# Stores of y and loads of the base x on GpSimd's queue instead of SyncE's, in a hybrid encoder layer

## The chip, the cores and the metric

The kernel runs on one core of a Trainium2 chip. The time is the device time of one execution in microseconds (us). Five engines run their own instruction streams and meet at semaphores: PE (TensorE, matrix products), DVE (VectorE), ACT (ScalarE), POOL (GpSimd) and SP (SyncE, which in this kernel only issues transfers). A transfer (DMA) is issued by one of these engines and carried out by the core's 16 DMA engines; SP's transfers run in a hardware queue (q1 in the profile) and POOL's in a software queue (q0).

## What is computed

One layer of a streaming encoder for 1024 prompt tokens and 64 tokens of a second request, width 1024, everything in float32:

```python
h = _rms(x, lw['norm1_g'])
proj = h @ lw['w_in']
p_rwkv, q, k, v, qm, gates = jnp.split(proj, _split_points(IN_SIZES), axis=-1)
...  # three mixers: a recurrence (o_a), windowed attention (o_b), attention into 256 memory tokens (o_m)
br = jnp.einsum('btnc,ncd->btnd', jnp.stack([o_a, o_b, o_m], axis=2), lw['w_branch'])
gt = jax.nn.sigmoid(gates.reshape(B, T, N_BRANCH, D_MODEL))
x = x + jnp.sum(gt * br, axis=2) @ lw['w_out']
h = _rms(x, lw['norm2_g'])
a_in, u = jnp.split(h @ lw['w_up'], 2, axis=-1)
...  # causal depthwise convolution of width 3 over a_in gives c
x = x + (jax.nn.gelu(c) * u) @ lw['w_down']
```

The input x is needed twice: normed, at the start, and unchanged, as the base to which the product with w_out is added. The sum (x1 in the kernel, and "x" in the profile, which drops numbers) takes the product with w_down on top and is the output y.

## The kernel before

Activations lie with the 1024 features on 8 tiles of 128 partitions and the tokens along the row. The tokens go through in three groups (GROUPS): 384, 384 and 320. For each group all weights are streamed from HBM again, in units: a unit is one output tile of 128 features, its weights 128 x 1024 floats (512 KB; half of that for w_branch, three quarters for w_down_end). A product in float32 is made of three in the faster fp32r form: ACT makes w_hi, a rounded copy of the raw weights (L318), DVE makes w_lo = raw - w_hi (L476), and PE adds hi*hi, lo*hi and hi*lo (L300, L301, L302) into one of two banks of `sums`. When PE is through with a unit, DVE or ACT reads its bank and so frees it for the unit after the next.

A group goes through these stages: attention columns (pa), in group 0 memory keys and values (mk, mv), recurrence columns (pr), then gates and branches, in pairs: a gate unit (512 KB), whose bank ACT reads with a tanh (L332), and a branch unit (256 KB), whose bank DVE multiplies by it (L512). The first sixteen pairs are for two branches (branch_first, branch), the last eight for the branch of the recurrence (branch_last), which needs the recurrence's result oa_hi, oa_lo (L1966, L1951). In the last eight pairs DVE adds to `merged` (L555) and ACT (L358) and DVE (L558) split it into mg_hi, mg_lo. Then the product with w_out (wo), 22 pairs with w_up (up_a, up_u), and 8 tiles with w_down, three units each (wd). DVE adds a finished tile of wo or wd to x1 (L516, L537).

Weights pass through a ring of four buffers `raw`. SP loads unit u + 3 when PE has finished unit u - 1 (`load`, L238): so a load is issued as PE starts a unit, and its data is wanted three units later. ACT's split of unit u + 2 stands in ACT's program ahead of what ACT does for the unit just finished.

The order of every engine is written out by hand: `in_order` (L2046) interleaves the steps of the small stages (norm, keys, attention, recurrence, base) with half units of the dense products, in the same way for each engine. Each engine holds only its own instructions, so an engine with nothing in a stretch goes on to its next instruction and waits there.

The lines in question:

- `store` in `dense_sync` (L241): after a tile's last w_down unit SP waits until DVE has added it to x1 (L244) and stores 128 x T floats of y (L245), T being the group's tokens. It stands behind the load of a later unit. There are 24 stores, of 192 KB in groups 0 and 1 and 160 KB in group 2.
- `base_sync` (L1970): SP waits for the group's last oa_lo and loads x again into x1, in four transfers of two tiles each (L1975; 384 KB, in group 2 320 KB). Its steps are interleaved with the last units of the gates, between the loads of their weights. DVE waits for all four ahead of wo (L515).
- `keys_pool` and `keys_in` (L837, L801): at the start of groups 1 and 2 POOL waits for the last store of y (L843), fills the attention's bias with a constant (L845) and loads the bias and the memory's keys and values (L816, L821, L824): 8 x 96 KB and 2 x 512 KB, in group 2 also 2 x 64 KB of cache.
- `end_sync` (L2028): SP stores two small outputs (o_cp, o_cs), behind all stores of y, and waits for the last transfers.

Of the kernel before, what the change touches and what calls it, by code (L numbers as in the profile page):

```python
# [45 lines left out]
GROUPS = ((0, 384), (384, 384), (768, 320))  # L46
# [142 lines left out]
def halves(n):  # L189
    return 2 if n.kt > 4 else 1  # L190
# [15 lines left out]
def freed(c, acc):  # L206

    return c.S["sum_free0" if acc % 2 == 0 else "sum_free1"], acc // 2 + 1
# [6 lines left out]
def raw_of(c, u):  # L215
    return c.raw[u % RAW_RING][:, 0:c.units[u].kt * P]
# [6 lines left out]
def lo_of(c, u):  # L223
    return c.w_lo[u % RAW_RING][:, 0:c.units[u].kt * P]


def dense_sync(sp, c):
    S = c.S
    loaded = [S[f"loaded{s}"] for s in range(RAW_RING)]

    def load(u):
        n = c.units[u]
        if u >= RAW_RING:
            sp.wait_ge(S["w_used"], u - RAW_RING + 1)
        dst = raw_of(c, u)
        if n.kind == "mv":
            dst = dst.rearrange("p (k m) -> p k m", k=2)
        sp.dma_start(dst, n.src).then_inc(loaded[u % RAW_RING], 16)  # L238

    def store(u):  # L240
        n = c.units[u]  # L241
        start = GROUPS[n.g][0]
        if n.kind == "wd" and n.ends:
            sp.wait_ge(*freed(c, n.acc))  # L244
            sp.dma_start(c.a["o_y"][:, n.m, start:start + n.T], c.x1[:, n.m, 0:n.T]).then_inc(S["y_out"], 16)  # L245

    for u in range(RAW_RING - 1):
        load(u)
    yield
    prev = None  # L250
    for u in c.sequence:
        if u is None:
            if prev is not None:
                store(prev)
            prev = None
            yield
            continue
        if u + RAW_RING - 1 < len(c.units):
            load(u + RAW_RING - 1)
        if halves(c.units[u]) == 2:  # L260
            yield
        if prev is not None:
            store(prev)
        prev = u
        yield


# [153 lines left out]
def dense_pool(pool, c):  # L421
    S = c.S

    def split(u):
        if u < len(c.units) and c.units[u].splitter == "pool":
            pool.wait_ge(S["w_hi"], u + 1)
            pool.tensor_tensor(lo_of(c, u), raw_of(c, u), hi_of(c, u).bitcast(F32), ALU.subtract).then_inc(S["w_lo_pool"], 1)

    def early(u):
        n = c.units[u]  # L430
        g, m, T = n.g, n.m, n.T
        i = FT * g + m
        if n.kind == "up_u":
            h = c.h[i % 2]
            pool.wait_ge(S["gelu"], i + 1)
            pool.wait_ge(*freed(c, n.acc))
            for tok, col in conv_parts(g):
                ins = pool.tensor_tensor(h[:, tok], h[:, tok], c.gl[i % 2][:, col], ALU.mult)  # L438
            ins.then_inc(S["h_made"], 1)
        if n.kind != "up_a":  # L440
            return
        raw = c.a_raw[i % 2]
        pool.wait_ge(*freed(c, n.acc))
        if g < LAST:
            pool.tensor_copy(c.conv_carry[:, 2 * m:2 * m + 2], raw[:, T:T + 2]).then_inc(S["carried"], 1)
        else:
            pool.tensor_copy(c.conv_carry[:, 2 * m:2 * m + 2], raw[:, PROMPT_END:PROMPT_END + 2])
            pool.tensor_copy(c.conv_last[:, 2 * m:2 * m + 2], raw[:, T + 2:T + 4]).then_inc(S["carried"], 1)

    split(0)  # L450
    split(1)
    yield
    prev = None
    for u in c.sequence:
        if u is None:
            if prev is not None:
                early(prev)
            prev = None
            yield
            continue  # L460
        if prev is not None:
            early(prev)
        if halves(c.units[u]) == 2:
            yield
        split(u + 2)
        prev = u
        yield
# [777 lines left out]
def idle(n):  # L1245
    for _ in range(n):
        yield
# [719 lines left out]
    yield from idle(2)  # L1967


def base_sync(sp, c, g):  # L1970

    start, T = GROUPS[g]
    sp.wait_ge(c.S["oa_lo"], 4 * (g + 1))
    for k in range(0, DT, 2):
        sp.dma_start(c.x1[:, k:k + 2, 0:T], c.a["xT"][:, k:k + 2, start:start + T]).then_inc(c.S["base_in"], 16)  # L1975
        yield


# [247 lines left out]
def build(nc, a):  # L2226
    c = Consts()
    c.a = a
    with ExitStack() as k:
        allocate(nc, c, k)  # L2230
        c.units, c.sequence = dense_units(c)
        c.acc = {(n.kind, n.g, n.m): n.acc for n in c.units if n.ends}
        block = k.enter_context(nc.Block())
        nothing = lambda steps: lambda g: idle(steps)

        def recurrence(eng, prep, inverse, state, post):
            def steps(g):
                yield from prep(eng, c, g)
                yield from scan(g, lambda p: inverse(eng, c, p), lambda p: state(eng, c, p))
                yield from post(eng, c, g)  # L2240
            return steps

        def together(eng, one, other):
            def steps(g):
                beside = other(eng, c, g)
                for _ in one(eng, c, g):
                    next(beside)
                    yield
            return steps

        def of(eng, step):
            return lambda g: step(eng, c, g)

        silent = lambda steps: lambda eng, c, g: idle(steps)

        @block.sync
        def _(sp):
            in_order(dense_sync(sp, c), {
                "first": lambda: first_sync(sp, c), "ready": lambda: idle(1), "start": lambda: start_sync(sp, c), "norm": of(sp, norm_sync), "memory": of(sp, memory_sync),
                "keys": nothing(KEY_STEPS), "attention": of(sp, attention_sync),  # L2260
                "recurrence": recurrence(sp, prep_sync, silent(INVERSE_STEPS), silent(STATE_STEPS), post_sync),
                "base": of(sp, base_sync), "norm2": nothing(1), "end": lambda: end_sync(sp, c)})

        @block.tensor
        def _(pe):
            in_order(dense_pe(pe, c), {
                "first": lambda: first_wait(pe, c), "start": lambda: idle(1), "ready": lambda: start_wait(pe, c), "norm": of(pe, norm_pe), "memory": of(pe, memory_pe),
                "keys": of(pe, keys_pe), "attention": of(pe, attention_pe),
                "recurrence": recurrence(pe, prep_pe, inverse_pe, state_pe, post_pe),
                "base": nothing(4), "norm2": of(pe, norm2_pe), "end": lambda: idle(1)})  # L2270

        @block.scalar
        def _(act):
            in_order(dense_act(act, c), {
                "first": lambda: first_wait(act, c), "start": lambda: idle(1), "ready": lambda: start_wait(act, c), "norm": of(act, norm_act), "memory": of(act, memory_act),
                "keys": of(act, keys_act), "attention": together(act, attention_act, mixing_act),
                "recurrence": recurrence(act, prep_act, inverse_act, state_act, post_act),
                "base": nothing(4), "norm2": of(act, norm2_act), "end": lambda: idle(1)})

        @block.gpsimd  # L2280
        def _(pool):
            in_order(dense_pool(pool, c), {
                "first": lambda: first_wait(pool, c), "start": lambda: idle(1), "ready": lambda: start_wait(pool, c), "norm": nothing(NORM_STEPS), "memory": nothing(MEM_STEPS),
                "keys": together(pool, keys_pool, keys_in), "attention": nothing(ATT_STEPS),
                "recurrence": recurrence(pool, prep_pool, inverse_pool, state_pool, silent(POST_STEPS)),
                "base": nothing(4), "norm2": nothing(1), "end": lambda: idle(1)})

        @block.vector
        def _(dve):
            in_order(dense_dve(dve, c), {  # L2290
                "first": lambda: first_wait(dve, c), "start": lambda: start_dve(dve, c), "ready": lambda: idle(1), "norm": of(dve, norm_dve), "memory": of(dve, memory_dve),
                "keys": of(dve, keys_dve), "attention": together(dve, attention_dve, mixing_dve),
                "recurrence": recurrence(dve, prep_dve, inverse_dve, state_dve, post_dve),
                "base": nothing(4), "norm2": of(dve, norm2_dve), "end": lambda: idle(1)})
# [144 lines left out]
```

## Time and profile before

| | us |
|---|---|
| median of 3 runs | 2136.65 |
| lowest and highest of them | 2132.02, 2137.83 |
| the profiled execution's own time | 2132.67 |
| its span in the trace | 2130.9 |

| engine | busy us | share of the span |
|---|---|---|
| PE | 2066.4 | 97% |
| DVE | 1264.5 | 59% |
| ACT | 945.4 | 44% |
| POOL | 165.6 | 8% |

The span is what the trace covers; the execution's own time holds 1.8 us more around it. Engine names with a q (SPq, POOLq) are an engine's queue of instructions that issue transfers. "To landing" is the time from the issue of a transfer until its semaphore has its full count. PE's matmuls overlap each other, so their busy times are merged in the share of the span. A window's row gives its width, then for each of PE, PEld (the weight load into the array), DVE, ACT and POOL the busy time and in brackets the number of instructions.

### The profile page before, as it was taken

What the parts mean: (1) busy time and instruction counts of PE and PEld (TensorE: products, weight loads), DVE (VectorE), ACT (ScalarE), POOL (GpSimd) and SP (SyncE); (2) the same over time, 40 slices, a digit from 0 to 9 for tenths busy, and PEclk for the clock granted to TensorE, in tenths of its full rate; (3) what the DMA queues carried; (4) which work ended last, traced back from release to release, by engine and by line L of the source; (5) the groups of instructions that cost most, each with busy time, mean ns of one, the idle gap of its engine ahead of it and who ended that gap; (6) DMA issues with size and microseconds to landing.
All of it is one profiled execution on the core that took longest, in us unless ns stands there. A gap on an engine that the chain in (4) does not pass through costs nothing.

```text
span 2130.9 us, 41128 instructions
## 1 busy us (share of the span) xinstructions
PE 2066.4 (97%) x17305; PEld 1963.6 (92%) x17305; DVE 1264.5 (59%) x2079; ACT 945.4 (44%) x1563; POOL 165.6 (8%) x268
## 2 busy tenths in 40 slices
PE   6999999999999999999999999999899999999999
PEld 5888899899999998889989999999888898999999
DVE  5566654656666545774446666654466645677753
ACT  5566332445444435743333544443475333455442
POOL 2000001001111010001000011100100110011110
PEclk9999999999999999999999999999999999999999
DMA  5422211354445452231124444455433213544454
GB/s 179 125 92 78 67 60 51 94 166 120 128 129 155 143 172 70 75 90 47 57 72 151 124 126 129 129 155 149 149 94 85 74 47 84 160 141 151 153 150 135
DMA packets 95959, 242.63 MB, mean 114 GB/s; under 512 B 24320, under 2 KB 35712, under 8 KB 95776
## 3 DMA queue, kind: packets, MB, share of 16 engines
q1 hardware_dynamic: 93984, 235.42, 36.9%
q0 software_dynamic: 1792, 4.59, 0.8%
q8 instruction: 137, 2.24, 0.4%
q14 instruction: 46, 0.38, 0.1%
HBM read 233.88 MB, written 6.09 MB: 113 GB/s over the span
## 4 chain that ended last, share of the span: by engine, by line
PE 87%; DVE 6%; ACT 3%; issue 2%; DMA 1%; SPq 0%; DVEq 0%; ACTq 0%
PE sums L300 24%; PE sums L302 23%; PE sums L301 23%; PE px L1491 5%; DVE w_lo L476 1%; PE px L1504 1%; PE ps_o L1041 1%; PE ps_o L1036 1%; PE pz L1767 1%; PE ps_t L1019 1%; PE ps_s L1005 1%; PE ps_s L1002 1%; DVE s L1120 1%; ACT w_hi L318 1%; PE ps_x L969 1%
## 5 line engine op out<-in xcount | busy, mean ns | idle before, releaser
L300 PE MATMUL sums<-x_hi,w_hi 128*128 128x384 f32 (+1 forms) x2208 | 742.3, 336 | 19.4 <-DVE x_lo L721 7.3
L302 PE MATMUL sums<-x_hi,w_lo 128*128 128x384 f32 (+1 forms) x2208 | 724.3, 328 | 0.0
L301 PE MATMUL sums<-x_lo,w_hi 128*128 128x384 f32 (+1 forms) x2208 | 724.2, 328 | 0.0
L476 DVE TENSOR_TENSOR w_lo<-raw,w_hi 128x1024 fp32r<-128x1024 f32 (+2 forms) x449 | 524.0, 1168 | 303.4 <-ACT w_hi L318 302.8
L318 ACT ACTIVATE w_hi<-raw 128x1024 fp32r<-128x1024 f32 (+1 forms) x452 | 441.0, 976 | 499.2 <-PE sums L302 273.4
L300 PEld LDWEIGHTS sums<-x_hi,w_hi 128*128 128x128 f32 x2208 | 417.7, 189 | 43.6 <-issue 29.4
L301 PEld LDWEIGHTS sums<-x_lo,w_hi 128*128 128x128 f32 x2208 | 418.5, 190 | 1.4
L302 PEld LDWEIGHTS sums<-x_hi,w_lo 128*128 128x128 f32 x2208 | 418.2, 189 | 0.0
L300 PE MATMUL sums<-h_hi,w_hi 128*128 128x384 f32 (+1 forms) x528 | 172.5, 327 | 0.0
L302 PE MATMUL sums<-h_hi,w_lo 128*128 128x384 f32 (+1 forms) x528 | 172.0, 326 | 0.0
L301 PE MATMUL sums<-h_lo,w_hi 128*128 128x384 f32 (+1 forms) x528 | 172.0, 326 | 0.0
L300 PE MATMUL sums<-o_hi,w_hi 128*128 128x384 f32 (+2 forms) x416 | 140.9, 339 | 4.8 <-DVE merged L512 3.6
L302 PE MATMUL sums<-o_hi,w_lo 128*128 128x384 f32 (+2 forms) x416 | 135.8, 326 | 0.0
L301 PE MATMUL sums<-o_lo,w_hi 128*128 128x384 f32 (+2 forms) x416 | 135.5, 326 | 0.0
L300 PEld LDWEIGHTS sums<-h_hi,w_hi 128*128 128x128 f32 x528 | 99.1, 188 | 0.2
L301 PEld LDWEIGHTS sums<-h_lo,w_hi 128*128 128x128 f32 x528 | 99.1, 188 | 0.2
L302 PEld LDWEIGHTS sums<-h_hi,w_lo 128*128 128x128 f32 x528 | 99.1, 188 | 0.0
L300 PEld LDWEIGHTS sums<-o_hi,w_hi 128*128 128x128 f32 x416 | 78.4, 189 | 10.5 <-issue 7.7
L438 POOL TENSOR_TENSOR h<-h,gl 128x384 f32<-128x384 f32 (+1 forms) x88 | 67.6, 779 | 231.5 <-DVE h L535 216.3
L365 ACT ACTIVATE gl<-cv 128x384 f32<-128x384 f32 (+1 forms) x66 | 33.6, 508 | 116.6 <-DVE cv L577 116.6
L577 DVE SCALAR_TENSOR_TENSOR cv<-a_raw,k_vecs,cv 128x384 f32<-128x384 f32 (+1 forms) x132 | 78.4, 594 | 2.3
L301 PEld LDWEIGHTS sums<-o_lo,w_hi 128*128 128x128 f32 x416 | 78.7, 189 | 0.7
(307 smaller groups left out, 2513.8 us busy)
## 6 DMA issues: line engine op xcount, KB each, us to landing
raw<-w_up SPq DMA_DIRECT2D x132, 512.0 KB, 3.6
raw<-w_gate SPq DMA_DIRECT2D x72, 512.0 KB, 3.6
raw<-w_down SPq DMA_DIRECT2D x48, 512.0 KB, 3.6
raw<-w_rwkv SPq DMA_DIRECT2D x42, 512.0 KB, 3.6
raw<-w_branch SPq DMA_DIRECT2D x72, 256.0 KB, 2.7
raw<-w_attn SPq DMA_DIRECT2D x30, 512.0 KB, 4.0
raw<-w_out SPq DMA_DIRECT2D x24, 512.0 KB, 3.6
raw<-w_down_end SPq DMA_DIRECT2D x24, 384.0 KB, 3.1
```

Source lines behind the costliest of these rows:

```text
L300: pe.matmul(out, wh[:, ws], n.hi[:, k, :], start=(n.begins and k == 0), stop=False)
L301: pe.matmul(out, wh[:, ws], n.lo[:, k, :], start=False, stop=False)
L302: mm = pe.matmul(out, wl[:, ws], n.hi[:, k, :], start=False, stop=(n.ends and k == n.kt - 1))
L318: act.activation(hi_of(c, u), raw_of(c, u), ACT.Copy).then_inc(S["w_hi"], 1)
L365: act.activation(c.gl[i % 2][:, 0:w], c.cv[i % 2][:, 0:w], ACT.Gelu_apprx_tanh).then_inc(S["gelu"], 1)
L438: ins = pool.tensor_tensor(h[:, tok], h[:, tok], c.gl[i % 2][:, col], ALU.mult)
L476: dve.tensor_tensor(lo_of(c, u), raw_of(c, u), hi_of(c, u).bitcast(F32), ALU.subtract).then_inc(S["w_lo_dve"], 1)
L577: dve.scalar_tensor_tensor(cv, raw[:, tap:tap + w], vec(c, "conv_w", 3 * m + tap), cv, ALU.mult, ALU.add).then_inc(S["conv"], 1)
L969: mm = pe.matmul(c.ps_x[0:nq, at:at + n], c.q_sq[:, i, tok], rhs, start=True, stop=True)
L1002: mm = pe.matmul(c.ps_s[0:p.nq, e, jj * 256 + cols.start:jj * 256 + cols.stop], c.q[H[e], 2 * p.r + jj, tok], c.kw[H[e], at + cols.start:a ...
L1005: mm = pe.matmul(c.ps_s[0:p.nq, e, jj * 256:jj * 256 + 256], c.q[:, 4 + 2 * e + jj, tok], c.mk[:, int(p.sample), 2 * e + jj, :], start=Tru ...
L1491: mm = eng.matmul(out[H[u], h * CHUNK:(h + 1) * CHUNK], tok(lhs, u, h), tok(rhs, u, h), start=True, stop=True)
```

## The change

The stores of y leave SP's program for POOL's, at the same place of the hand-written order; the loads of the base x do the same. Each keeps its wait. SP keeps the loads of weights, the next group's x for its norm, the tables and the small outputs.

```diff
 def dense_sync(sp, c):
...
-    def store(u):
-        n = c.units[u]
-        start = GROUPS[n.g][0]
-        if n.kind == "wd" and n.ends:
-            sp.wait_ge(*freed(c, n.acc))
-            sp.dma_start(c.a["o_y"][:, n.m, start:start + n.T], c.x1[:, n.m, 0:n.T]).then_inc(S["y_out"], 16)
...
@@ dense_pool
+    def store(u):
+        n = c.units[u]
+        start = GROUPS[n.g][0]
+        if n.kind == "wd" and n.ends:
+            pool.wait_ge(*freed(c, n.acc))
+            pool.dma_start(c.a["o_y"][:, n.m, start:start + n.T], c.x1[:, n.m, 0:n.T]).then_inc(S["y_out"], 16)
...
         if prev is not None:
             early(prev)
+            store(prev)
...
-def base_sync(sp, c, g):
+def base_in(pool, c, g):
 
     start, T = GROUPS[g]
-    sp.wait_ge(c.S["oa_lo"], 4 * (g + 1))
+    pool.wait_ge(c.S["oa_lo"], 4 * (g + 1))
     for k in range(0, DT, 2):
-        sp.dma_start(c.x1[:, k:k + 2, 0:T], c.a["xT"][:, k:k + 2, start:start + T]).then_inc(c.S["base_in"], 16)
+        pool.dma_start(c.x1[:, k:k + 2, 0:T], c.a["xT"][:, k:k + 2, start:start + T]).then_inc(c.S["base_in"], 16)
         yield
...
@@ block.sync
-                "base": of(sp, base_sync), "norm2": nothing(1), "end": lambda: end_sync(sp, c)})
+                "base": nothing(4), "norm2": nothing(1), "end": lambda: end_sync(sp, c)})
@@ block.gpsimd
-                "base": nothing(4), "norm2": nothing(1), "end": lambda: idle(1)})
+                "base": of(pool, base_in), "norm2": nothing(1), "end": lambda: idle(1)})
```

## Rows read from the trace of the kernel before

**Rows 1.** The page, part 1: busy time, share of the span, instructions.

```profile
PE 2066.4 (97%) x17305; PEld 1963.6 (92%) x17305; DVE 1264.5 (59%) x2079; ACT 945.4 (44%) x1563; POOL 165.6 (8%) x268
```

**Rows 2.** Windows, six stretches: width, busy us (count) per engine, clock, DMA, GB/s.

```profile
400.00:437.00 37.00, 37.00 (x208) 35.93 (x207) 24.48 (x40) 13.97 (x23) 0.00 (x0) 1.00 0.35 110
...
1154.00:1190.00 36.00, 35.91 (x206) 35.51 (x205) 21.66 (x32) 16.45 (x26) 0.00 (x0) 1.00 0.57 179
...
1390.00:1487.00 97.00, 97.00 (x561) 96.84 (x560) 48.00 (x66) 36.07 (x48) 1.50 (x3) 1.00 0.51 153
1487.00:1520.00 33.00, 31.35 (x211) 30.73 (x210) 14.06 (x20) 15.24 (x20) 8.69 (x13) 1.00 0.69 208
...
1815.00:1843.00 28.00, 26.54 (x179) 26.04 (x179) 17.25 (x29) 12.13 (x21) 0.00 (x0) 1.00 0.49 141
1843.00:1870.00 27.00, 25.10 (x168) 24.27 (x167) 16.45 (x25) 12.24 (x20) 0.00 (x0) 1.00 0.63 195
```

**Rows 3.** Timeline of DVE, group 0: start, duration, engine, line, operation.

```profile
406.66 1.96 DVE L1951 TENSOR_TENSOR oa_lo<-ar,oa_hi 128x384 fp32r<-128x384 f32 x4
```

**Rows 4.** Timeline of DVE, group 2, the same step.

```profile
1816.62 1.69 DVE L1951 TENSOR_TENSOR oa_lo<-ar,oa_hi 128x320 fp32r<-128x320 f32 x4
```

**Rows 5.** Timeline of SP's queue, group 0 (start, issue time).

```profile
412.17 0.33 SPq L238 DMA_DIRECT2D raw<-w_gate  x1
...
420.50 0.33 SPq L238 DMA_DIRECT2D raw<-w_branch  x1
...
437.54 0.43 SPq L1975 DMA_DIRECT2D x<-xT  x1
```

**Rows 6.** Timeline of ACT, group 0; in brackets the idle time before.

```profile
415.79 1.06 ACT L318 ACTIVATE w_hi<-raw 128x1024 fp32r<-128x1024 f32 x1 [2.54 <-DMA raw<-w_gate]
...
419.57 0.47 ACT L332 ACTIVATE th<-sums 128x384 f32<-128x384 f32 x1
```

**Rows 7.** DMA issues at 400 to 437: count, KB each, median us to landing.

```profile
raw<-w_gate SPq DMA_DIRECT2D x5, 512.0 KB, 3.5
```

**Rows 8.** Timeline of POOL, start of group 1.

```profile
774.19 4.70 POOL L816 DMA_DIRECT2D bias<-alibi  x8 [0.59 <-POOL bias L845]
...
779.45 0.56 POOL L824 DMA_DIRECT2D mv<-o_mv  x1
```

**Rows 9.** Timeline of DVE, the same stretch.

```profile
775.18 1.22 DVE L476 TENSOR_TENSOR w_lo<-raw,w_hi 128x1024 fp32r<-128x1024 f32 x1 [1.20 <-ACT w_hi L318]
```

**Rows 10.** DMA issues at 780 to 784 (issued at 781.73).

```profile
raw<-w_attn SPq DMA_DIRECT2D x1, 512.0 KB, 5.8
```

**Rows 11.** DMA issues at 784 to 788 (issued at 785.89).

```profile
raw<-w_attn SPq DMA_DIRECT2D x1, 512.0 KB, 4.4
```

**Rows 12.** DMA issues at 1496 to 1500 (issued at 1496.88).

```profile
raw<-w_attn SPq DMA_DIRECT2D x1, 512.0 KB, 6.7
```

**Rows 13.** Chain that ended last, 1815 to 1872: start, duration, what.

```profile
1820.89 3.54 DMA raw<-w_gate
...
1849.38 4.21 DMA raw<-w_gate
```

**Rows 14.** Timeline of PE in that stretch.

```profile
1828.66 0.39 PE L300 MATMUL sums<-x_hi,w_hi 128*128 128x320 f32 x1 [0.76 <-ACT th L332]
```

**Rows 15.** Tile bias, 770 to 900: ns min/median/max, first and last start.

```profile
L1120 DVE SCALAR_TENSOR_TENSOR s<-ps_s,q_y,bias x24: 473/476/485, 826.7 to 891.3; 128x256 f32<-128x256 f32 x24
```

**Rows 16.** Timeline at the end, all engines.

```profile
2127.46 0.49 DVE L537 TENSOR_TENSOR x<-sums,x 128x320 f32<-128x320 f32 x1 [7.49 <-PE sums L302]
...
2128.84 0.45 SPq L2032 DMA_DIRECT2D o_cs<-conv_last  x1
```

**Rows 17.** DMA issues at 2127.9 to 2128.3.

```profile
o_y<-x SPq DMA_DIRECT2D x1, 160.0 KB, 1.8
```

**Rows 18.** DMA issues at 2098 to 2129.

```profile
o_cs<-conv_last SPq DMA_DIRECT2D x1, 22.0 KB, 1.6
```

**Rows 19.** Tile bias, whole span, loads by POOL: us to landing.

```profile
DMA to landing us min/median/max: 2.7/3.8/5.4
```

More of the change, by code:

```diff
@@ L249, in dense_sync @@
     yield
-    prev = None
     for u in c.sequence:
         if u is None:
-            if prev is not None:
-                store(prev)
-            prev = None
             yield
@@ L261, in dense_sync @@
             yield
-        if prev is not None:
-            store(prev)
-        prev = u
         yield
@@ L462, in dense_pool @@
             early(prev)
+            store(prev)
         if halves(c.units[u]) == 2:
```

## The prediction

> **What bounds the kernel now.** I read the page's busy times first, then windows stage by stage, then, for the stages that the change touches, the chain of waits and the timelines. PE is busy for 2066.4 of 2130.9 us [rows 1], so a change off PE's path can win only where PE idles. The windows show where that is [rows 2]: in the w_down stage, where y is stored, PE idles 0 of 97 us (all three groups read 97.00). In the stage with the base loads it idles 0.09 us of 36 in group 1 (group 0 alike), but in group 2 1.46 of 28 us just before the loads and 1.90 of 27 during them. With 320 tokens PE needs less time for the same weights, and there the transfers set the pace: the chain runs through the landing of w_gate, 3.54 us after its issue [rows 13], then ACT's split, DVE's w_lo, the merge, and ACT's tanh that frees PE's bank; the next gate unit waited 0.76 us for that tanh [rows 14].
>
> **The change part by part.**
>
> *What leaves SP.* 24 stores and 12 base loads, each an issue of 0.33 to 0.43 us [rows 5]. SP's loads wait for PE to be done with an old buffer, and between two of them SP stands still for longer than an issue. So this frees nothing that PE waits for: 0.
>
> *The stores in the w_down stage, on POOL.* POOL has nothing else there (1.50 us busy of 97, PE full [rows 2]). A POOL issue takes 0.56 to 0.59 us (8 in 4.70) [rows 8]. The data of a store now shares the DMA engines with a weight load instead of standing behind it in one queue, which may delay that load a little; PE has no idle time in the stage, and its loads are wanted three units later. I take 0. DVE might be held while POOL issues: w_lo took 1.22 us in the middle of eight POOL issues [rows 9], its usual time, so 0 again. Behind the last store of a group POOL now fills the bias and loads it later, by about 0.25 us for the longer issue and 0.5 for the slower landing. The bias is first read at 826.7 [rows 15], its loads are issued from 774.19 [rows 8] and take 5.4 us at most [rows 19], so some 40 us cover this. The shift moves POOL's burst of bias and memory loads against w_attn's, a stretch where PE idles 1.65 of 33 us in group 2 [rows 2]; it may cost or give back up to 1.5 us, and I take 0.
>
> *The base loads on POOL.* This is the real move. SP issued them paced by PE, one to a unit, from 437.54 [rows 5], each behind a weight load in the same queue. POOL has no pace: in the gate stage it has no instruction (0.00 us, x0, from 400 to 437 [rows 2]), so it waits at the last oa_lo and issues all four at once. That wait ends in group 0 at 406.66 + 1.96 = 408.62 [rows 3], 29 us earlier than before. Nothing behind it on POOL is due before w_up, and DVE wants the data only at w_out, so early does no harm to them. But 4 x 384 KB now arrive in some 2.4 us of issues, in a separate queue, beside the loads of w_gate and w_branch.
>
> How much can a gate load be late? In group 0 the next one is issued at 412.17 [rows 5]. It landed by 415.79, when ACT split it; behind that hang w_lo, the merge, the next split and the tanh, which ended at 419.57 + 0.47 = 420.04 [rows 6]. PE ended the unit before at 420.50, when SP's next load was released [rows 5]. So 0.46 us are to spare; beyond, every late microsecond is PE's. Group 2 has nothing to spare [rows 14].
>
> How late will it be? The nearest rows are POOL's bursts at the start of groups 1 and 2: 8 x 96 and 2 x 512 KB from 774.19 to 780.0 [rows 8]. Loads of the same 512 KB from SP took 5.8 us when issued 1.7 us after the last of these issues, 4.4 us when issued 5.9 us after it, and at worst, between the two largest, 6.7 us [rows 10 to 12]; undisturbed, w_gate takes 3.5 [rows 7]. The base burst is smaller (1.5 MB against 1.8) and its last issue ends about 1.2 us ahead of the gate load. I take 5.2 us in groups 0 and 1, between the rows of 4.4 and 5.8 and nearer to the second: 5.2 - 3.5 - 0.46 = 1.2 us each. Only one gate load a group is hit: the next follows a pair of units later, some 6 us. In group 2 the wait ends at 1818.31 [rows 4], POOL's issues at about 1820.7, and the gate load goes out at 1820.89 [rows 13], closer: I take 5.5, with no spare 2.0 us. Against that, the old base loads no longer delay the gate load at 1849.38, which took 4.21 [rows 13]: minus 0.7. Net 1.3 us. Lower bound of the part: no load is delayed, 0 + 0 - 0.7; upper: each takes 6.7, 2 x 2.7 + 3.2 - 0.7 = 7.9.
>
> The Trainium skill has a rule for this, in "DMA: Bandwidth & Descriptors", "Queues, rings and completion order": each DMA engine takes turns between the queues that have work for it, a packet at a time. By it a gate load beside a burst gets half of the engines: if 2 of its 3.5 us are fixed (the page's fit, in "Anatomy of one DMA — SWDGE (gpsimd) path"), the other 1.5 double, and it lands after 5.0 us, an estimate; the sum of the three groups would be 1.0 + 1.0 + 0.8 = 2.8 us against 3.7. The rows of 5.8 and 6.7 lie above it, so the trace decides.
>
> *The end.* DVE ends the last tile at 2127.46 + 0.49 = 2127.95; SP then issued the store (landing after 1.8 us [rows 17]), and o_cp and o_cs behind it; o_cs ended the run, issued at 2128.84 [rows 16] and landed 1.6 later [rows 18], at 2130.44, 0.46 before the end of the span. Now o_cp and o_cs go out earlier, and POOL's store ends it. A landing of POOL's issues takes 2.7 us at least, 3.8 in the median, for 96 KB in busy stretches [rows 19]; the quiet store from SP took 1.8. I take 2.5: 2127.95 + 2.5 + 0.46 = 2130.9, so 0; bounds 1.8 and 3.8 give -0.7 and +1.3.
>
> By the Trainium skill, in that same section of "DMA: Bandwidth & Descriptors", 2.0 us and the bytes at 436 GB/s, the 160 KB land after 2.4 us, an estimate, and the end would come 0.1 earlier; no row here shows a quiet POOL store.
>
> *Sum:* 1.2 + 1.2 + 1.3 + 0 = 3.7 us; bounds -0.7 - 0.7 - 1.5 = -2.9 and 7.9 + 1.3 + 1.5 = 10.7. The profiled execution took 2132.67 us, 3.98 less than the median of the runs, whose times fall into one at 2132 and two near 2137. I add the sum to the middle of the two, 2134.7, and forecast 2138.4.
>
> **The rivals.**
>
> *A, the transfers hide anyway.* The burst's data is over before the gate load's begins, or POOL's transfers start so slowly that a gate load hardly notices. For it: the engines are busy only 35% of the time from 400 to 437 [rows 2], and the burst's issues end before the gate load's issue. Against: the landings of 5.8 and 6.7 [rows 10, 12], and a gate load has less spare than w_attn. Then 0 + 0 - 0.7 and the end: about -0.7, 2134.0. The Trainium skill, "DMA: Bandwidth & Descriptors", "Issuing engines are not separate DMA queues", goes this way: issuing from several engines saves only the issue time. The trace agrees as far as the issue time is hidden here, but not that the pace stays the same.
>
> *B, the freed stretch runs faster.* All that PE idles where base loads and weights shared SP's queue, 2 x 0.09 + 1.46 + 1.90 [rows 2], and 0.7 at the end come back: -4.2, 2130.5. Against: the 1.46 are lost before any base load is issued, so they have another cause.
>
> *C, slower: the burst holds w_gate for its full length.* Place: the gate load behind POOL's four issues, in each group. If it takes 6.7 us, as the worst row [rows 12], PE waits 2.7 + 2.7 + 3.2 - 0.7 and the end adds 1.3: +9.2, 2143.9. For it: that row, and 1.65 us that PE lost right behind it [rows 2]. Against: that load lay between two transfers of 512 KB, this one lies behind the last issue. It counts as slower from landings of about 6.2 us on.
>
> That the base loads keep their old times is no rival: nothing on POOL holds them until 437.
>
> **How the numbers follow.** Chances: forecast 0.50, A 0.29, B 0.05, C 0.16. A run of this kernel can be told from no change at about 0.3%, 6.4 us. The forecast's own range is 2134 to 2143. The range reaches down to A on the lower of the two levels, about 2131, and up to C with some of the spread of the runs, 2146. Faster by over 0.3%: B alone comes near, 0.03. Slower: most of C and a little of the forecast, 0.15. The rest, 0.82, is within 0.3%.
>
> **What would show it.** In the changed trace POOL issues four base loads back to back once a group, at about 408.7 in group 0 and 1818.4 in group 2; the next w_gate load lands after 5 to 6 us instead of 3.5, and PE waits for ACT's tanh once behind it, for about 1 us. In the w_down stage PE stays at 97.00 of 97. At the end o_cp and o_cs come before the last tile, and a POOL store is last. I am wrong if that gate load lands within 4 us (A), if it takes over 6.2 (C), or if PE idles in the w_down stage.

## The result, and the profile after

The changed kernel is slower: 2152.59 us in the median of six runs (2150.75 to 2155.34) against 2135.58 for the kernel before in the same rounds. The ratio is 1.0083 with a 95% interval of 1.0073 to 1.0093, a loss of 17.0 us between the medians. The prediction was 2138.4 with a range up to 2146.0 and a chance of 0.15 for slower by over 0.3%; the time lies outside the range.

The profiled execution took 2155.34 us, the longest of the six, with a span of 2153.5. Part 1 of its page, beside [rows 1]: PE is busy 8.2 us longer with the same 17305 instructions, so its matmuls have become slower, and that is not all of the loss.

```profile
PE 2074.6 (96%) x17305; PEld 1971.1 (92%) x17305; DVE 1265.0 (59%) x2079; ACT 945.3 (44%) x1563; POOL 189.7 (9%) x304
```

**The base loads.** POOL's timeline of the changed kernel in groups 0 and 2 (start, duration, engine, line, idle time before). The four loads go out back to back when oa_lo is done, as predicted, though each takes 0.73 us to issue and not 0.58.

```profile
409.48 2.92 POOL L1970 DMA_DIRECT2D x<-xT  x4 [39.26 <-DVE oa_lo L1946]
...
1831.16 2.93 POOL L1970 DMA_DIRECT2D x<-xT  x4 [45.28 <-DVE oa_lo L1946]
```

The DMA issues from 412 to 414 of the changed kernel (KB each, us to landing). The load of w_gate, issued at 412.74, took 6.8 us, where [rows 7] have 3.5.

```profile
raw<-w_gate SPq DMA_DIRECT2D x1, 512.0 KB, 6.8
```

The chains of waits that hold the same load in groups 1 and 2 of the changed kernel (start, duration), where [rows 13] have 3.54 and 4.21:

```profile
1136.11 6.33 DMA raw<-w_gate
```

```profile
1833.45 7.65 DMA raw<-w_gate
```

Three windows of the changed kernel show why (columns as in [rows 2]; the last two are the DMA engines' busy share and GB/s). From 412 to 418 the engines are full. The burst, this gate load and the branch load behind it are 1536 + 512 + 256 KB, 2.36 MB; at some 340 GB/s, from these rows, that is 6.9 us of work, an estimate, and the gate load lands when nearly all of it is done.

```profile
412.00:414.00 2.00, 2.00 (x14) 2.00 (x13) 1.44 (x3) 1.01 (x2) 0.40 (x1) 1.00 0.96 346
414.00:416.00 2.00, 2.00 (x13) 2.00 (x12) 0.71 (x2) 0.00 (x0) 0.00 (x0) 1.00 1.03 320
416.00:418.00 2.00, 2.00 (x13) 2.00 (x13) 0.00 (x0) 0.00 (x0) 0.00 (x0) 1.00 0.92 362
```

**The chain to PE.** ACT's timeline in the changed kernel: the split waits 5.77 us for the load, against 2.54 in [rows 6], and the tanh that frees PE's bank comes at 423.36 instead of 419.57.

```profile
419.59 1.06 ACT L304 ACTIVATE w_hi<-raw 128x1024 fp32r<-128x1024 f32 x1 [5.77 <-DMA raw<-w_gate]
...
423.36 0.47 ACT L318 ACTIVATE th<-sums 128x384 f32<-128x384 f32 x1
```

PE's timeline in the three groups of the changed kernel: the pause in brackets, and the first matmul behind it, which in group 2 takes 0.61 us against the 0.39 of [rows 14].

```profile
423.97 0.55 PE L286 MATMUL sums<-x_hi,w_hi 128*128 128x384 f32 x1 [2.94 <-ACT th L318]
...
1146.85 0.41 PE L286 MATMUL sums<-x_hi,w_hi 128*128 128x384 f32 x1 [2.45 <-ACT th L318]
...
1845.33 0.61 PE L286 MATMUL sums<-x_hi,w_hi 128*128 128x320 f32 x1 [4.87 <-ACT th L318]
```

Windows of the changed kernel behind each pause; the column ahead of the DMA share is the granted clock. It is about 0.50 (1.2 GHz) for some three us in groups 0 and 1 and six in group 2, and 1.00 (2.4 GHz) again afterwards; the windows of four us take in some of that. The time lost by it is the busy time by one minus the clock: 1.7 + 1.6 + 2.8 = 6.1 us, on top of the pauses' 2.94 + 2.45 + 4.87 = 10.3.

```profile
424.00:428.00 4.00, 4.00 (x14) 4.00 (x15) 2.89 (x5) 1.30 (x2) 0.00 (x0) 0.57 0.02 4
...
1147.00:1151.00 4.00, 4.00 (x15) 4.00 (x16) 2.77 (x5) 1.18 (x2) 0.00 (x0) 0.59 0.00 0
...
1845.00:1851.00 6.00, 5.67 (x22) 5.70 (x23) 3.10 (x5) 1.60 (x3) 0.00 (x0) 0.51 0.01 3
```

**The w_down stage** with its stores on POOL, a window of the changed kernel: PE is full, as in the 97.00 of [rows 2].

```profile
678.00:776.00 98.00, 98.00 (x566) 97.73 (x565) 49.78 (x66) 37.90 (x49) 5.65 (x11) 1.00 0.51 155
```

**The end.** The changed kernel's last rows of the timeline, where [rows 16] had a store by SP:

```profile
2146.45 0.49 DVE L532 TENSOR_TENSOR x<-sums,x 128x320 f32<-128x320 f32 x1 [7.38 <-PE sums L288]
2147.24 0.54 POOL L420 DMA_DIRECT2D o_y<-x  x1 [8.71 <-DVE x L532]
```

This store landed after 2.1 us, at 2149.3. The span goes on to 2153.5, since the program's end (L2224, the close of the block; L2229 before) has a DRAIN on POOL's queue. Instructions of that line, first in the changed kernel, then in the kernel before (durations in ns; first and last start):

```profile
L2224 POOLq DRAIN  x1: 6029/6029/6029, 2147.2 to 2147.2; - x1
```

```profile
L2229 POOLq DRAIN  x1: 4256/4256/4256, 2050.7 to 2050.7; - x1
```

Before, POOL was through with its program at 2050.7, and its 4.26 us lay beside the w_down stage. Now 6.03 us stand behind the last store. From the last tile's end to the end of the span (the tail, below) it was 2130.9 - 2127.95 = 2.95 us; now it is 2153.5 - 2146.94 = 6.6.

The account of the two profiled spans, 22.6 us apart: pauses 10.3, less the 0.76 that group 2 had before [rows 14], clock 6.1, end 3.6, together 19.2. Most of the other 3.4 us can be found too. Summed over windows of 2 us, PE's busy time by one minus the clock is 29.5 us after and 21.5 before, so the clock costs 8.0 us more, 1.9 of them away from the three pauses: for example behind a wait of 2.15 us for the recurrence's table from_rows at 1810.08, where before a wait of 2.12 us at 1799.10 left the clock at 1.00. And in the attention of group 2, where a load of w_attn now takes 7.63 us (at 1511.45), PE's pauses for DVE's q add up to 3.15 us against 2.38. The medians are only 17.0 us apart.

### The profile page after: what moved, and what is told of

The parts are those of the page before. It is cut to its first block, busy times and chain, and to the rows that moved or that the text cites. A ratio compares the mean times of both kernels' runs of the same rounds, so it can differ in the third digit from the quotient of the medians.

```text
span 2153.5 us, 41128 instructions
## 1 busy us (share of the span) xinstructions
PE 2074.6 (96%) x17305; PEld 1971.1 (92%) x17305; DVE 1265.0 (59%) x2079; ACT 945.3 (44%) x1563; POOL 189.7 (9%) x304
## 4 chain that ended last, share of the span: by engine, by line
PE 85%; DVE 6%; ACT 3%; DMA 2%; issue 2%; SPq 0%; POOLq 0%; POOL 0%; DVEq 0%; ACTq 0%
PE sums L286 23%; PE sums L288 22%; PE sums L287 22%; PE px L1486 5%; DMA raw<-w_gate 1%; DVE w_lo L471 1%; ACT w_hi L304 1%; PE px L1499 1%; PE ps_o L1036 1%; PE ps_t L1014 1%; PE pz L1762 1%; PE ps_s L1000 1%; PE ps_o L1031 1%; PE ps_s L997 1%; PE ps_x L964 1%
```

## The experiments

My theory was that the price is the burst, because POOL has no pace, and that the end adds the rest; the rivals were the software queue itself and the bytes brought early. Base and stores were parted first. All ratios are to the kernel before, timed on the same chip in the same rounds, with their 95% interval; the microseconds behind them are differences of the medians, which can differ from the ratio by a few tenths.

**stores_only**: the base loads go back to SP.

```diff
-                "base": of(pool, base_in), ...        # POOL
+                "base": of(sp, base_sync), ...        # SP, paced by its weight loads
```

> Stores of y on GpSimd's queue, base loads back on SyncE's. Theory (the four base loads in one burst make a w_gate load late in each group, PE stands still over 2 us and then runs at half its clock; the stores cost nothing but the end): the three stalls behind w_gate are gone, what stays is the end, 3 to 4 us longer because GpSimd's drain of 6.0 us follows the last store; time about 2139, 3 to 4 us over before. Rival (GpSimd's software queue slows the weight loads wherever it runs, the 24 stores too): PE idles in the w_down stage, and at least half of the 17 us stay, 2144 or more.

2138.1 against 2133.59 us, 1.0018 (1.0009 to 1.0027): 4.5 us. No gate load was late. The end line of this kernel, behind a last tile done at 2132.31 in a span of 2137.9:

```profile
L2224 POOLq DRAIN  x1: 5051/5051/5051, 2132.6 to 2132.6; - x1
```

The tail is 5.6 us instead of 2.95. For the other 1.9 us the profiled execution has a candidate, not a shown cause: PE waits 3.04 us for the recurrence's table at 1802.13 (2.12 before) and runs at half the clock for some three us behind it. last_store_on_sync, below, has 23 of the same stores and waits 1.97 us there.

**base_only**: the base loads on POOL, the stores still on SP.

> Base loads on GpSimd's queue, stores of y back on SyncE's. Theory: the three stalls stay (w_gate landing 6.3 to 7.6 us after its issue, PE idle 2.5 to 5 us each, clock 0.5 for 3 to 5 us after), the end is as before; about 13 to 15 us over before, 2149 to 2151. Rival (stores carry half of the loss): 2144 or less.

2147.26 against 2133.59, 1.0062 (1.0040 to 1.0084): 13.7 us, within the 13 to 15 over before that I expected, though the time lies below 2149, as the kernel before stood lower in these rounds. The gate loads took 6.3, 6.8 and 6.5 us, and PE paused 2.42, 2.91 and 3.68 us. The tail stayed at 2.9 us. PE's timeline and a window behind the first pause:

```profile
421.66 0.66 PE L300 MATMUL sums<-x_hi,w_hi 128*128 128x384 f32 x1 [2.42 <-ACT th L332]
```

```profile
421.66:425.00 3.34, 3.34 (x11) 3.34 (x12) 2.58 (x5) 1.32 (x2) 0.00 (x0) 0.50 0.03 9
```

So two parts, 13.7 + 4.5 = 18.2 us, make up the 17.0 of the whole, within the noise (the interval of base_only alone is 8.5 to 17.9 us).

**base_paced**: base_only, but POOL waits, ahead of each load, for the unit at which SP had issued it. It parts POOL's queue as such from the pace.

```diff
     pool.wait_ge(c.S["oa_lo"], 4 * (g + 1))
-    for k in range(0, DT, 2):
+    last = last_of(c, "branch_last", g) - 1
+    for k, v in zip(range(0, DT, 2), (last - 3, last - 2, last, last + 1)):
+        pool.wait_ge(c.S["w_used"], v - RAW_RING + 1)
         pool.dma_start(...)
```

> Base loads on GpSimd's queue but each held until PE reaches the unit at which SyncE issued it in the kernel before; stores on SyncE's queue. Theory (the pace is what was lost, not the queue): the w_gate loads land after 3.5 to 4.5 us, no stall of over 1 us, time within 3 us of before, 2134 to 2139. Rival (a transfer in the software queue beside a weight load delays it by itself, since it no longer stands behind it): gate loads at 5 to 6 us in the last two pairs of each group and 2142 or more.

2132.53 against 2133.59, 0.9997 (0.9987 to 1.0008). POOL's timeline shows the loads apart, and a window shows PE full:

```profile
437.01 0.75 POOL L1977 DMA_DIRECT2D x<-xT  x1 [68.06 <-PE sums L302]
438.83 0.73 POOL L1977 DMA_DIRECT2D x<-xT  x1 [1.06 <-PE sums L302]
445.07 0.72 POOL L1977 DMA_DIRECT2D x<-xT  x1 [5.51 <-PE sums L302]
449.23 0.72 POOL L1977 DMA_DIRECT2D x<-xT  x1 [3.44 <-PE sums L302]
```

```profile
400.00:440.00 40.00, 40.00 (x225) 38.85 (x224) 25.79 (x41) 14.85 (x26) 1.48 (x2) 1.00 0.41 117
```

The same loads on the same queue, without the burst, cost nothing. The queue is not the price.

**burst_on_sync**: the four loads at oa_lo, but issued by SP in its own queue.

```diff
+def base_now(sp, c, g):
+    sp.wait_ge(c.S["oa_lo"], 4 * (g + 1))
+    for k in range(0, DT, 2):
+        sp.dma_start(c.x1[:, k:k + 2, 0:T], ...).then_inc(c.S["base_in"], 16)
...
     yield from idle(POST_STEPS)
+    base_now(sp, c, g)
```

> Base loads stay on SyncE's queue, but all four are issued back to back as soon as the last oa_lo is there, as GpSimd did. Theory (the burst fills the DMA engines; in one queue it stands ahead of the gate load, in two they share): burst of 1.5 MB ahead of the next w_gate, which lands after 4.5 to 6 us instead of 6.3 to 7.6, PE idles 0.5 to 2 us a group, 2138 to 2143. Rival A (only the bytes matter, whichever the queue): w_gate lands after 6.3 us or more and the loss is that of GpSimd's burst, 2149. Rival B (only the software queue hurts): w_gate within 4 us and 2135.

2149.88 against 2133.59, 1.0075 (1.0058 to 1.0092): 16.3 us. My expectation failed; the time is that of rival A, though w_gate itself landed after 5.9 us and it is the branch load ahead of it that is late. A burst costs no less on SP's queue. SP's timeline, ACT's and PE's, and a window:

```profile
404.48 0.33 SPq L238 DMA_DIRECT2D raw<-w_gate  x1
407.26 1.92 SPq L1976 DMA_DIRECT2D x<-xT  x4
409.23 0.47 SPq L238 DMA_DIRECT2D raw<-w_branch  x1
```

```profile
415.48 0.63 ACT L318 ACTIVATE w_hi<-raw 128x512 fp32r<-128x512 f32 x1 [6.31 <-DMA raw<-w_branch]
```

```profile
416.63 0.66 PE L300 MATMUL sums<-x_hi,w_hi 128*128 128x384 f32 x1 [3.79 <-ACT th L332]
```

```profile
420.00:421.00 1.00, 1.00 (x5) 1.00 (x4) 0.56 (x1) 0.08 (x1) 0.00 (x0) 0.50 0.00 0
```

Here it is the branch load right behind the four, half the size, that lands after 6.2 us. SP's program also holds it back: in base_only it goes out 2.1 us behind its gate load, which here would be at 406.6, and it goes out at 409.23, behind SP's wait for oa_lo and 1.92 us of issues. So some 2.6 us of its delay are no matter of the transfers, and 13.7 and 16.3 us are not made up alike; what the run shows is that the loss needs neither POOL nor its queue. The Trainium skill, "DMA: Bandwidth & Descriptors", "Issuing engines are not separate DMA queues", says that transfers from all engines end up on the same 16 DMA engines and mix there; the landings agree, 6.2 us behind SP's own burst and 6.3 beside POOL's.

**two_and_two**: base_only, with two loads at oa_lo and two when PE is done with the second unit of branch_last (the + 6 in the diff is the unit that SP loads at that point); all bytes still come early and from POOL.

```diff
+    later = first_of(c, "branch_last", g) + 6
     for k in range(0, DT, 2):
+        if k == 4:
+            pool.wait_ge(c.S["w_used"], later - RAW_RING + 1)
         pool.dma_start(...)
```

> Base loads on GpSimd's queue, two at once at the last oa_lo and two more when PE is done with the second branch unit of the recurrence; stores on SyncE's queue. Theory (a burst costs only beyond what a gate load has to spare, and a pause of over 2 us costs as much again in the clock): the gate load behind each half lands after 4 to 5 us, PE idles at most 1 us a time, the clock stays at 1.00, 2133 to 2138. Rival (the loss goes with the bytes that come at once): half of 13.7 us is left, 2140 or more.

2133.07 against 2133.35, 1.0000 (0.9991 to 1.0009). POOL's timeline, the gate load issued behind the first two, a window of PE, and PE's largest pause, in group 2, at a clock of 1.00 behind it:

```profile
407.66 1.48 POOL L1978 DMA_DIRECT2D x<-xT  x2 [39.27 <-DVE oa_lo L1951]
419.51 1.44 POOL L1978 DMA_DIRECT2D x<-xT  x2 [10.38 <-PE sums L302]
```

```profile
raw<-w_gate SPq DMA_DIRECT2D x1, 512.0 KB, 3.9
```

```profile
405.00:440.00 35.00, 35.00 (x201) 34.60 (x200) 20.13 (x31) 13.04 (x22) 2.92 (x4) 1.00 0.59 175
...
1828.00:1829.00 1.00, 1.00 (x7) 1.00 (x8) 0.62 (x2) 0.98 (x1) 0.00 (x0) 1.00 0.91 286
```

```profile
1827.97 0.38 PE L300 MATMUL sums<-x_hi,w_hi 128*128 128x320 f32 x1 [1.78 <-ACT th L332]
```

Half of the burst at a time costs not half of the price but nothing that can be measured. In groups 0 and 1 the gate load still lands within its spare time. In group 2, which has none, it took 4.6 us, and the pause of 1.78 us, 0.76 before, is longer than the 1 us that I expected, but the clock stayed up.

**tanh_again**: does the pause itself lower the clock, or do the full DMA engines? The kernel before, with one tanh on the chain repeated 4, 8 and 12 times in all in groups 0, 1 and 2 (the same values again); no transfer is changed.

```diff
+            if c.units[u + 1].kind == "branch_last" and m == 3:
+                for k in range((3, 7, 11)[g]):
+                    act.activation(c.th[i % 2][:, 0:T], bank(c, n), ACT.Tanh, scale=0.5).then_inc(S["again"], 1)
+                    act.wait_ge(S["again"], (0, 3, 10)[g] + k + 1)
             act.activation(c.th[i % 2][:, 0:T], bank(c, n), ACT.Tanh, scale=0.5).then_inc(freed(c, n.acc)[0], 1)
```

> The kernel before, with ACT's tanh at the fourth gate of the recurrence's branch computed 4, 8 and 12 times over in groups 0, 1 and 2 (the same values again), so PE must wait for its bank with no transfer changed. Theory (the clock falls because PE stood still, whatever the reason): PE idles about 1, 3 and 5 us; behind the first the clock stays 1.00, behind the second and third it reads 0.5 for 3 us or more, and those two stalls cost nearly twice their length; in all 13 to 17 us over before, 2147 to 2151. Rival (the clock falls through the transfers' load, not through the pause): 1.00 behind all three, and 8 to 9 us over before, 2142.

2148.15 against 2133.35, 1.0073 (1.0058 to 1.0089): 14.8 us. PE's timeline at the three pauses, and windows behind them:

```profile
434.79 0.41 PE L300 MATMUL sums<-x_hi,w_hi 128*128 128x384 f32 x1 [1.25 <-ACT th L336]
...
1157.24 0.41 PE L300 MATMUL sums<-x_hi,w_hi 128*128 128x384 f32 x1 [3.45 <-ACT th L336]
...
1853.07 0.60 PE L300 MATMUL sums<-x_hi,w_hi 128*128 128x320 f32 x1 [5.77 <-ACT th L336]
```

```profile
436.00:437.00 1.00, 1.00 (x8) 1.00 (x7) 0.77 (x1) 0.20 (x1) 0.00 (x0) 1.00 0.02 8
...
1159.00:1160.00 1.00, 1.00 (x5) 1.00 (x4) 0.77 (x2) 0.20 (x1) 0.00 (x0) 0.50 0.00 0
...
1853.00:1857.00 4.00, 3.93 (x15) 3.96 (x16) 2.61 (x4) 1.34 (x2) 0.00 (x0) 0.50 0.00 0
```

A pause of 1.25 us left the clock at 1.00; those of 3.45 and 5.77 were followed by 0.50, with no transfer under way (DMA share 0.00). The pauses make 10.5 us; the rest of the 14.8 is the slow clock behind two of them, 1.7 and 2.4 us by the windows.

**last_store_on_sync**: stores_only, with the one last store of y back on SP, behind o_cs.

```diff
 def end_sync(sp, c):
...
+    n = c.units[-1]
+    start = GROUPS[n.g][0]
+    sp.wait_ge(*freed(c, n.acc))
+    sp.dma_start(c.a["o_y"][:, n.m, start:start + n.T], c.x1[:, n.m, 0:n.T]).then_inc(S["stored"], 16)
```

> As the run with the stores alone on GpSimd's queue, but the last store of y is issued by SyncE. Theory (what the stores cost is GpSimd's drain behind its last transfer): the drain runs beside the last tile, the end is again about 3 us behind the last addition, and the time is within 2 us of before, 2132 to 2136. Rival (the 4.5 us of that run are spread over the stores or come from the later bias loads): 2137 or more.

2132.47 against 2133.35, 1.0001 (0.9991 to 1.0011). The DRAIN now starts beside the last tile, and the span ends at 2129.1, 2.2 us after SP's store:

```profile
2126.89 0.33 SPq L2031 DMA_DIRECT2D o_y<-x  x1
```

```profile
L2228 POOLq DRAIN  x1: 4969/4969/4969, 2117.8 to 2117.8; - x1
```

So 23 of the 24 stores on POOL cost nothing, and the last one is the price of stores_only.

**change_mended**: the whole change, with the base paced as in base_paced and the last store on SP.

> The whole change with its two costs taken out: base loads on GpSimd's queue, each held until PE reaches the unit at which SyncE issued it before; stores on GpSimd's queue, but for the last one on SyncE's. Theory (bursts and the drain are all that the change cost; 13.7 and 4.5 us, and nothing in between): within 2 us of before, 2131 to 2136. Rival (the two parts together cost something that neither shows alone): 2138 or more.

2133.56 against 2134.59, 0.9997 (0.9987 to 1.0007). The two causes are all of the loss; nothing is won either.

The DRAIN on POOL's queue in base_paced and in change_mended:

```profile
L2231 POOLq DRAIN  x1: 5237/5237/5237, 2049.1 to 2049.1; - x1
```

```profile
L2230 POOLq DRAIN  x1: 5951/5951/5951, 2118.4 to 2118.4; - x1
```

Across the runs its length goes with the transfers that POOL has issued in the whole program. It is 4.25 to 4.26 us where POOL issues neither stores nor base loads (before, burst_on_sync, tanh_again), 5.24 with the twelve base loads, in a burst or paced, 4.97 with 23 stores, 5.05 with 24, 5.95 with twelve and 23, and 6.03 with all. The parts add up, 4.26 + 0.98 + 0.79 = 6.03, though in base_only the last base load was issued over 200 us ahead of the DRAIN.

**paced_keys** and **paced_keys_bias** try the same on POOL's old burst at the start of groups 1 and 2, on top of base_paced: the first holds the memory's keys and values to later units of attention, the second the bias loads too.

```diff
+        pool.wait_ge(S["w_used"], first_of(c, "pa", g) + 6)      # + 5 in paced_keys
         pool.dma_start(c.mk[:, 0], ...)
...
+            if g:                                                # paced_keys_bias alone
+                pool.wait_ge(S["w_used"], first_of(c, "pa", g) + 1 + 2 * e + u)
             for r in range(2):
                 pool.dma_start(c.bias...)
```

> Base loads on GpSimd's queue paced as in the run before (2132.5), stores on SyncE's queue, and GpSimd's loads of the memory's keys and values at the start of groups 1 and 2 held until PE has done 5 and 8 attention units. Theory (this is the same kind of burst, with 1.6 us lost in group 2): the w_attn load that took 6.7 us lands within 5, PE's 1.5 us wait there goes, 2130 to 2132, 1 to 3 us under before. Rival (that wait has another cause, the bias loads or the units' own pace): no change, 2132.5 to 2134.

2130.61 against 2133.35, 0.9991 (0.9982 to 1.0000). My theory failed: a pause of 1.39 us in group 2 stayed (1.52 before), the next one grew from 0.86 to 1.64, and a w_attn load, issued some 12 us ahead of the first of the memory's loads, still took 6.2 us, so those did not delay it.

> As the run with paced base loads and paced memory keys and values, with the eight bias loads of groups 1 and 2 spread as well, two behind each of the first four attention units. Theory (what was left of the burst there was the bias: the w_attn load issued among its loads still took 6.2 us and PE still waited 1.4): no w_attn load over 5 us, no wait of over 0.5 us there, 1 us under that run, 2128 to 2131. Rival (the bias is too small to matter and that wait comes from the norm's or the cache's loads): no change, 2130 to 2133.

2131.94 against 2134.59, 0.9989 (0.9981 to 0.9998), 2.3 us by the ratio: the one version whose interval lies below 1, if barely, and among ten versions one such interval is weak evidence. That pause fell from 1.52 us before to 0.54:

```profile
1499.96 0.38 PE L300 MATMUL sums<-x_hi,w_hi 128*128 128x320 f32 x1 [0.54 <-DVE q L498]
```

But two w_attn loads still took 5.3 and 5.4 us, where none over 5 was expected, and the pause behind it grew from 0.86 us (at 1521.48) to 1.98 (at 1520.35), so PE idles no less there, and where the 2.3 us come from stays open.

## Why the prediction was wrong, step by step

*What leaves SP, 0*: right. base_paced takes the base loads away from SP, change_mended also all but the last store, and neither gains anything that can be measured.

*Stores in the w_down stage, 0*: right; PE has 98.00 of 98, and last_store_on_sync is level.

*The place and time of the burst*: right, and so was the chain from the gate load to ACT's tanh. "POOL has no pace" is the cause, as base_paced against base_only shows: 0.9997 against 1.0062.

*The landing of the gate load* is the first step that failed. I took 5.2 and 5.5 us from [rows 10, 11]; it took 6.8, 6.3 and 7.65. I had put POOL's issues at 0.58 us for 96 KB loads, so that a 1.2 us gap was left to the gate load; at 0.73 us for 384 KB the gap in group 0 is 412.74 - 412.40 = 0.3. And I weighed only the 35% of busy time over the whole stretch (for rival A), when the burst fills the engines: 208 GB/s at a share of 0.69 [rows 2] make 300 at full engines, and 2.36 MB take 7.9 us at that rate. The row of 6.7 [rows 12] was the right neighbour; I kept it for rival C because it lay between two transfers. Taking turns between the queues (the Trainium skill, "DMA: Bandwidth & Descriptors", "Queues, rings and completion order") gave an estimate of 5.0 us, with a fixed part that the page has from POOL's transfers, and the load is SP's; the trace has 6.3 to 7.65, so it was further off than my own. With the measured landings my own formula gives pauses of 2.8 + 2.4 + 4.2 us; measured were 2.94, 2.45 and 4.87, the last with the 0.76 that stood there before. The formula was right and the landing was not: the pauses add 9.5 us where I had 4.4 ahead of the 0.7 taken off. That 0.7 did not come either: beside the pause PE idles 2.6 us in group 2's stretch (1815 to 1890), as before (1815 to 1870).

*"Beyond, every late microsecond is PE's"* is the second. Late microseconds cost more: 10.3 us of pauses were followed by 6.1 us lost at half the clock, a term that I had put at nothing by leaving it out. The measured landings alone would have left the forecast at about 2144, inside the range; either of the clock's 6.1 us and the end's 3.6 takes it out. Rival C had the mechanism, its place and a landing of 6.7, and priced it at 7.9 us, for want of the clock; base_only measures 13.7. tanh_again shows that a pause is enough for it, without a change to the transfers.

This could have been read beforehand, in the attention and recurrence of the kernel before, where I did not look, as the change doesn't touch them. PE's timeline of the kernel before, and windows behind these pauses:

```profile
834.45 1.10 PE L1019 MATMUL ps_t<-k_ident,p 128*128 128x128 f32 x8 [2.40 <-ACT p L1220]
...
1545.18 1.09 PE L1019 MATMUL ps_t<-k_ident,p 128*128 128x128 f32 x8 [3.06 <-ACT p L1220]
...
1658.47 0.38 PE L300 MATMUL sums<-o_hi,w_hi 128*128 128x320 f32 x1 [2.23 <-DVE merged L512]
```

```profile
836.00:838.00 2.00, 2.00 (x14) 2.00 (x13) 1.82 (x5) 2.00 (x8) 0.00 (x0) 1.00 0.00 0
...
1547.00:1549.00 2.00, 2.00 (x10) 2.00 (x9) 1.18 (x2) 2.00 (x8) 0.00 (x0) 0.50 0.04 8
...
1660.00:1662.00 2.00, 1.78 (x11) 1.38 (x13) 2.00 (x5) 0.00 (x1) 0.00 (x0) 0.50 0.00 0
```

Two of these three pauses are followed by 0.50. Had I carried the pauses of rival C with such a slow stretch behind each, it would have come nearer to the time.

*The bias and keys, 0 within 1.5*: 0.8 us more idle time in group 2 in the profiled run; within the bounds.

*The end, 0*, is the third: the landing was sized well, 2.1 us against 2.5, but the step left out POOL's DRAIN behind its last transfer. It could have been seen: it takes 4.26 us in the kernel before, hidden at 2050.7. It costs 2.65 us of tail in stores_only and 3.6 in the changed kernel, and putting one store back takes the ratio from 1.0018 to 1.0001. Its length, 4.3 to 6.0 us, goes with what POOL has issued; why is open, and so is the 1.9 us of stores_only outside its tail.

*Rivals*: A and B fell, the gate load being late in all groups. C was the right side and the right place, at half its price.

## What to carry to other kernels

A transfer that stands in one engine's program between paced loads is paced by them; moved to an engine with an emptier program it is issued as soon as its own wait allows, so lay the bytes then in flight against the rate of the DMA engines, and hold it with a wait if the sum is longer than the next load's spare time. When a change lets PE pause for a few microseconds, price the slow clock behind the pause as well as the pause. Before a transfer becomes an engine's last work, read what that engine still does at the end of the program, even where it is hidden now.

## What the runs showed of the hardware

- In the gate stage, where PE had been busy throughout, every pause from 2.42 to 5.77 us was followed by about three us or more at a granted clock of 0.50 (1.2 GHz), and those of 1.25 and 1.78 us by 1.00. In the attention of the kernel before a pause of 2.40 us was not, and ahead of the recurrence's table 2.15 us was (after) and 2.12 was not (before), so the length alone does not tell it. Full DMA engines are not needed for it.
- A load issued into a burst landed about when the burst did: in group 0 of the changed kernel at 419.5, its last base load at 419.1. Behind four of 384 KB (320 in group 2), issued by POOL or by SP, a 256 KB load took 6.2 us and a 512 KB load 5.9 to 7.65; with two ahead the 512 KB load took 3.9 and, in group 2, 4.6.
- POOL's DRAIN at the end of the program took 4.26 us before and 6.03 in the changed kernel; twelve base loads add 0.98 us to it and 24 stores 0.79, whenever they were issued. SP's took 7 ns in both.
- A base load of 384 KB takes POOL 0.73 us to issue, and SP 0.48 (four in 1.92).
